# Values product of the dilated attention: two half-array products per key tile, or one over the whole array for both heads

## The reference, cut to what matters

```python
DIL_GROUPS = ((128, 1), (512, 4), (2048, 16))     # window, dilation
for g, (window, dilation) in enumerate(DIL_GROUPS):
    radius = window // (2 * dilation)              # 64 keys to either side
    o, lse = dilated_window_attention(q[:, :, hs], k[:, :, hs], v[:, :, hs], dilation, radius, slopes[hs])
...
p = jnp.exp(s - lse[..., None]).astype(v.dtype)    # s is scores + ALiBi bias, masked
o = jnp.einsum("bdnqhk,bdnkhe->bdnqhe", p, vw)     # the values product
```

## Time and profile before

| | |
|---|---|
| median of 3 runs | 2651.08 us |
| lowest and highest | 2650.41 and 2653.76 us |
| span of the profiled execution, first to last instruction | 2647.7 us |
| its own time | not given apart from the span; the median is 3.4 us over the span |
| TensorE busy (matmul) | 2414.7 us, 91% |
| VectorE, ScalarE, GpSimd busy | 1235.3, 981.3, 444.2 us |

### The profile page before, as it was taken

The page is one execution under the profiler, slowest core; times in us unless marked ns, Lnnn a source line. Parts: engine busy times, 40 slices in busy tenths (PEclk is TensorE's granted clock), DMA queues, the critical chain, the costliest instruction groups (busy, mean ns, idle before and its releaser), DMA issues. The chain is left out here.

```text
span 2647.7 us, 38172 instructions
## 1 busy us (share of the span) xinstructions
PE 2414.7 (91%) x14495; PEld 2089.8 (79%) x14495; DVE 1235.3 (47%) x1813; ACT 981.3 (37%) x1644; POOL 444.2 (17%) x306
## 2 busy tenths in 40 slices
PE   5999998999799999999899798069999999999997
PEld 4876665666688888888788687069999999999997
DVE  6334345445423320000244434956666666666663
ACT  6333333434500011211300222135565555655653
POOL 0001101110200000000000000023434434344342
PEclk7999998998999999999899899579999999999998
DMA  5300000001011112222344443268788887888872
GB/s 167 104 24 25 17 24 17 17 25 40 2 47 40 40 31 83 90 89 89 104 153 146 170 159 116 90 196 257 235 257 250 261 256 233 258 249 264 254 234 64
DMA packets 328236, 342.67 MB, mean 129 GB/s; under 512 B 11856, under 2 KB 308816, under 8 KB 327632
## 3 DMA queue, kind: packets, MB, share of 16 engines
q1 hardware_dynamic: 315280, 309.96, 37.3%
q0 software_dynamic: 12864, 31.46, 4.5%
HBM read 297.35 MB, written 44.04 MB: 129 GB/s over the span
## 5 line engine op out<-in xcount | busy, mean ns | idle before, releaser
L1977 PE MATMUL bank_pair<-tokens_hi_lo,ehi 128*128 128x320 f32 x2048 | 534.0, 347 | 1.1 <-DVE tokens_hi_lo L1843 1.1
L1978 PE MATMUL bank_pair<-tokens_hi_lo,elo 128*128 128x160 f32 x2048 | 483.9, 236 | 0.0
L1978 PEld LDWEIGHTS bank_pair<-tokens_hi_lo,elo 128*128 128x128 f32 x2048 | 392.5, 192 | 0.0
L1977 PEld LDWEIGHTS bank_pair<-tokens_hi_lo,ehi 128*128 128x128 f32 x2048 | 385.7, 188 | 1.2 <-issue 1.2
L1778 ACT ACTIVATE ehi<-eraw 128x2048 fp32r<-128x2048 f32 x192 | 366.2, 1907 | 10.8 <-DMA eraw<-in_w_eg 7.9
L1836 DVE TENSOR_TENSOR elo<-eraw,ehi 128x2048 fp32r<-128x2048 f32 x144 | 329.2, 2287 | 82.7 <-ACT ehi L1778 82.7
L1754 POOL TENSOR_TENSOR elo<-eraw,ehi 128x2048 fp32r<-128x2048 f32 x47 | 224.8, 4783 | 388.2 <-ACT ehi L1778 388.2
L1977 PE MATMUL bank_pair<-hidden_hi_lo,ehi 128*128 128x320 f32 x1024 | 271.6, 348 | 19.1 <-DVE hidden_hi_lo L1849 19.1
L1978 PE MATMUL bank_pair<-hidden_hi_lo,elo 128*128 128x160 f32 x1024 | 241.4, 236 | 0.0
L1977 PEld LDWEIGHTS bank_pair<-hidden_hi_lo,ehi 128*128 128x128 f32 x1024 | 191.9, 187 | 23.4 <-DVE hidden_hi_lo L1849 22.1
L1206 PE MATMUL bank_pair<-hT_hi,whi 128*128 128x512 f32 (+1 forms) x576 | 204.0, 354 | 1.2 <-PEq L1036 1.2
(11 more groups left out here) (245 smaller groups left out, 4365.0 us busy)
## 6 DMA issues: line engine op xcount, KB each, us to landing
eraw<-in_w_eg SPq DMA_DIRECT2D x64, 1024.0 KB, 7.3
eraw<-in_w_eu SPq DMA_DIRECT2D x64, 1024.0 KB, 5.4
eraw<-in_w_ed SPq DMA_DIRECT2D x64, 1024.0 KB, 5.3
raw<-in_w_in SPq DMA_DIRECT2D x64, 512.0 KB, 4.1
scratch_g<-sig SPq DMA_DIRECT2D x24, 640.0 KB, 3.4
sig<-scratch_g SPq DMA_DIRECT2D x24, 640.0 KB, 3.9
xt<-in_x SPq DMA_DIRECT2D x10, 512.0 KB, 4.6
scratch_m<-acc SPq DMA_DIRECT2D x8, 640.0 KB, 4.9
```

The lines of the kernel that those rows point to most:

```text
L1977: nc.tensor.matmul(out, wh, moving[:, k, :], start=(k == 0), stop=False)
L1978: ins = nc.tensor.matmul(out[:, HI], wl, moving[:, k, HI], start=False, stop=(k == KD - 1))
```

## The change

Four places change, all in the attention stage.

1. `pv`: for each key tile one matmul with the tile's 128 columns (both heads' channels) as the stationary operand, all 128 partitions, and 256 moving columns, the 128 queries of head 0 and of head 1 (`PT[:, c:4:2, :]`, two runs of 128 that lie 256 elements apart). It writes 128 by 256 of `obank`, of which the two diagonal quarters are wanted.
2. `o_copy`: two activations of 64 partitions, each from the quarter of its head.
3. `v_copy`: a tile with 64 keys gets zeros in its other 64 partitions (24 tiles over the six phases).
4. VectorE clears both PT buffers once at the start of the stage, so that rows which were never written hold numbers.

```diff
@@ o_copy, ScalarE
-                    nc.scalar.activation(dst, obank[:, 0:P], ACT.Copy).then_inc(o_copied, 1)
+                    for h in range(2):
+                        r = slice(64 * h, 64 * h + 64)
+                        ins = nc.scalar.activation(dst[r], obank[r, h * P:(h + 1) * P], ACT.Copy)
+                    ins.then_inc(o_copied, 1)
@@ v_copy, VectorE
                 for a, (i, _, _, ln) in enumerate(tl):
+                    if ln < P:
+                        nc.vector.memset(V[m % 2][ln:P, i, :], 0.0)
                     ins = nc.vector.tensor_copy(V[m % 2][0:ln, i, :], src[0:ln, a, :])
@@ VectorE, start of the stage
             split_lo(0)
+            for pt in PT:
+                nc.vector.memset(pt[:], 0.0)
@@ pv, TensorE
-                for h in range(2):
-                    if un["att"]:
-                        for c, (i, _, _, ln) in enumerate(un["keys"]):
-                            ins = nc.tensor.matmul(obank[64 * h:64 * h + 64, 0:P],
-                                                   V[un["buf"]][0:ln, i, 64 * h:64 * h + 64],
-                                                   PT[v % 2][0:ln, 2 * h + c, :], start=(c == 0),
-                                                   stop=(c == len(un["keys"]) - 1))
-                    else:
+                if un["att"]:
+                    n_keys = len(un["keys"])
+                    for c, key_tile in enumerate(un["keys"]):
+                        ins = nc.tensor.matmul(obank[:, 0:2 * P], V[un["buf"]][:, key_tile[0], :],
+                                               PT[v % 2][:, c:4:2, :], start=(c == 0), stop=(c == n_keys - 1))
+                else:
+                    for h in range(2):
```

## The result

The changed kernel takes 2657.27 us (median of 12 runs, 2652.37 to 2662.22) and the kernel before, on the same chip, 2651.58 (12 runs, 2650.41 to 2653.76). The ratio is 1.0018, with a 95% interval of 1.0010 to 1.0027: it is slower by about 0.2%, where 2637 was forecast. The profiled execution has a span of 2656.1 us.

A forecast was written before the change was run, and what follows sets the result against it. TensorE, busy for 91% of the span, was taken as the bound. Product -21.5, evacuation +2.4, gains lost in waits +2.8 and zeros +2.1 gave -14.2 us, from 2651.1 to 2637 us; the range ended at 2648.

The forecast's parts named there:

- The product: Values product: mixed-tile units gain 18.7 us, full units cost 0.8, single-tile units gain 3.6; 21.5 us off TensorE in all.
- Neither rival on the product: Values product: idle times stay, about 2651 us, chance 0.09; or the two-run moving operand reads slowly, 2695 us, chance 0.05.
- the entry gap: TensorE's idle 0.20 us before a unit's values product, forecast to shrink by 0.10 us per unit (0 to 0.20).
- The gains that run into the wait for the copy: Denominators' transposes on TensorE wait for ScalarE's copy behind the exponentials, so 2.8 us of the gain is lost.
- The evacuation: ScalarE's second activation adds 0.16 us; 15 of 60 units show it ahead of the denominators' transpose: 2.4 us.
- The zeros for V: VectorE's clearings among the value copies, 0.15 us each; 14 of 24 lie in TensorE's waits: 2.1 us (1.5 to 3.1).
- the clock only as a width: TensorE's stretches at 1.2 GHz, about 33 us in the stage, could shift the time a few us either way.
- Clearing PT: Two VectorE operations at the stage's start, hidden behind 5.3 us of TensorE matmuls: nothing, up to 2.4 us uncovered.
- The third rival: All 60 second activations on ScalarE lie on the path at 0.38 us, costing 22.8 us: 2657 us, chance 0.03.
- The signs named in advance: Wrong if a pass took 0.3 us or more, idle times stayed, or TensorE's waits in the stage grew over 12 us.
- The rule that the prediction set against itself: Matmuls on different column groups run concurrently, so the whole-array product gains nothing: -1.1 us, some 2654 us with the additions.

The follow-up runs named there:

- experiment 5: The changed kernel with one evacuation of 128 partitions and the zeros written by GpSimd ahead of each phase: 2636.67 us against 2651.93 for the kernel before.
- experiment 6: The changed kernel, both evacuations kept, with the zeros written by GpSimd instead of VectorE: 2646.88 us, ratio 0.9982.
- experiment 1: The kernel before with only the evacuation changed, two activations of 64 partitions in place of one of 128: 2659.75 us against 2651.36.
- experiment 2: The kernel before with only VectorE's zeros added, for the 24 short value tiles and both PT buffers: 2660.12 us, ratio 1.0031.
- experiment 9: The changed kernel with two evacuations, zeros on GpSimd, and ScalarE's values' copies ahead of the exponentials: 2635.78 us against 2651.85 for the kernel before.
- experiment 7: The kernel before with half-array products over all 128 rows, one evacuation and zeros written by GpSimd: 2635.73 us, ratio 0.9932.
- experiment 10: The kernel before with only ScalarE's order changed, the values' copy ahead of the newly scored unit's exponentials: 2645.46 us, ratio 0.9975.
- experiment 8: The kernel of experiment 7 with ScalarE's values' copy ahead of the newly scored unit's exponentials: 2627.89 us, ratio 0.9904 to the kernel before.
- experiment 11: The kernel before with the evacuation cut by queries, two activations of 128 partitions by 64: 2652.83 us, ratio 1.0002.
- experiment 3: The changed kernel with the old single evacuation of 128 partitions, product and VectorE's zeros kept: 2647.43 us, ratio 0.9984 to the kernel before.
- experiment 4: The kernel before with half-array products over all 128 rows of each value tile, one evacuation, zeros on VectorE: 2644.57 us, ratio 0.9974.

## Why the prediction was wrong

The balance, all from medians: product -15.3 (experiment 5), second activation +10.2 (5 to 6), VectorE's zeros +10.4 (6 to the change), together +5.3 us. The measured difference is +5.7. That they add up is no test, since each step starts where the last one ended; the test is that the additions cost much the same alone, 8.4 us (experiment 1) and 8.8 us (experiment 2).

- *The product* was right in kind, and its size was off by two errors that partly cancel. Two-tile units take 1.10 us at the median from their start to L859 (0.98 to 1.21), single units 0.66, and the idle time ahead of the segment's first weight load is 0.026 us in place of 0.17. Neither rival on the product came: the gaps did not stay, and a pass of 256 columns stays at 0.22 us. But 21.5 us were priced from one unit of each kind, and over all units it is 16.7 (experiment 5): where a full unit took 0.82 to 0.94 us, the new one takes up to 0.24 more, not 0.17, and the entry gap shrinks from 0.20 to 0.11 us in 37 of 60 units, not in all.
- *The gains that run into the wait for the copy* were put at 2.8 us; the listed waits of experiment 5 are only 0.6 us longer than before. So -21.5 + 2.8 = -18.7 was forecast for the product with one evacuation and -15.3 measured, with an interval (-20 to -12) that holds the forecast; that it comes so near is in part luck.
- *The evacuation* is the step that failed first. "0.16 us is what the second one adds" was read from a copy and a split that both start at partition 0. Two activations whose partitions differ do not overlap: the pair holds ScalarE 0.40 us longer per unit, and 0.6 with strided writes. Even the upper end (0.38) was too low for a strided pair, and the count too: 21 transposes fall due behind the copy, not 15, and what is queued on ScalarE behind the pair, the split of the weights above all, comes later as well (experiment 9). The forecast was 2.4 us, and 10.2 were measured.
- *The zeros for V* failed as much: 2.1 us were forecast and 10.4 measured. The count of 14 was right, the 0.15 us was near the operation's own 0.165. But on VectorE a zero also undoes the overlap of the copies on either side of it, so that it adds 0.33 us: 14 x 0.33 = 4.6 us of wait in place of 2.1, against 4.3 between the changed kernel and experiment 6 (14.6 and 10.3). The remaining 6 are mainly TensorE's clock, which falls to 1.2 GHz behind the longer waits; the forecast had the clock only as a width of a few us either way. The traces show the division: in these two kernels TensorE has the same instructions in the same order, and between 60 and 735 us the changed kernel's steps from start to start add up to 9.4 us more. Of these 4.2 lie at steps with a wait ahead, and 5.2 at steps without one in a stretch at 1.2 GHz.
- *Clearing PT* at nothing is consistent with the trace (two operations of 0.485 us from 55.9 us on); no run isolates it.
- *The third rival* gave 2657, which is the measured time, but by chance and another way: it had all 60 second activations on the path at 0.38. The runs show half the loss there and the other half at the zeros. Its objection, that ScalarE idles for most of the stage, was the error: an engine that idles for some 60% of the stage can still be the last thing that a chain waits for.
- *The signs named in advance* pointed right: TensorE's four largest waits in the stage grew from 27.3 (8.5 + 5.0 + 9.6 + 4.2) to 40.9 us, past the 12 us that were to show it wrong.
- *The rule that the prediction set against itself*, that two half-array products run side by side as fast as one over the array, holds once no tile has 64 rows: experiment 7 is as fast as experiment 5, and its product takes even less of TensorE.

The measured time lies above the range, whose upper end was 2648, because the ends of the two terms were taken from single instructions, not from the steps that the change makes of them. (The sum's own worst end is about -4 us and not -6 with the activation at its 0.38; that is still inside the range.) What stays open is what makes the clock fall: of the 16 waits of 1.95 us or more in the four kernels with zeros on VectorE, 11 go with a low stretch and 5 do not, and the time at the lower level also differs by a few us from one profile to another in stages that no run changes.

## What to carry to other kernels

An added instruction is priced by the step that it makes with its neighbours, not by its own duration or by the step of a like pair: where it starts at other partitions than the instruction ahead of it, take its whole duration and add the overlap that both neighbours lose. Where tiles of 64 rows between tiles of 128 cost gaps, zero rows under the same half-array products can bring the gain, as here, with the zeros on an engine that nothing waits for. And read the order of a queue: here the copy that frees an accumulator was worth 6 to 11 us (experiments 10, 8 and 9, each against the same kernel with the old order) when it stood ahead of work that could wait.

## What the runs showed of the hardware that was not expected

- On ScalarE, two activations that start at different partitions ran one after the other, 12 ns from end to start, also with the next instruction (24 ns): 0.27 us or a little more from the first's start to the second's, and 0.38 to 0.40 with strided writes, against 0.10 to 0.12 for two activations of all 128 partitions and half the columns (experiment 11).
- On VectorE a clearing of 64 partitions between copies added 0.33 us, twice its duration of 0.165. The same clearings on GpSimd take 0.20 us each, and with them the wait for the value copies is the 8.5 us of before (experiment 5).
- Where a wait in a dense stretch grew from 1.06 us to 1.95 or more, 3.4 us of TensorE at 1.2 GHz went with it in 11 of 16 cases (the changed kernel and experiments 2, 3 and 4), and never at the eight waits of 1.06 us of the kernel before.
- Padding the contraction with zero rows made float32 products faster: the 24 mixed units, four passes of 128 by 64 and four of 64 by 64, took 1.64 to 1.78 us to the segment's second matmul, and with eight passes of 128 by 64 they take 0.82 to 0.94 (experiments 4 and 7).
